# Gate and up weights of an expert block: one 2 MB request in place of two of 1 MB

## The reference, cut to what matters

```
def swiglu_2(t, w_gu, w_dn):
    g, u = jnp.split(t @ w_gu, 2, axis=-1)
    return (jax.nn.silu(g) * u) @ w_dn
...
    def one_block(args):
        rb, e = args
        return swiglu_2(t_pad[rb], w_gu[e], w_dn[e]).astype(jnp.float32)

    ys = lax.map(one_block, (rows.reshape(n_blk, EXPERT_BLOCK), blk_expert)).reshape(P, D)
```

## Time and profile before

| what | value |
|---|---|
| median of 3 runs | 3324.0 us (3318.94 to 3326.96) |
| profiled execution, its own time | 3329.74 us |
| span of the profiled execution | 3327.9 us |
| expert blocks | about 2560 to 3270 us of the span |
| requests of expert weights | 216 of 1 MB (72 for each of `big`, `h_buf`, `s_buf`) |
| DMA, whole span | 534.41 MB, mean 161 GB/s |
| TensorE clock granted | 0.994 of full speed |

### The profile page before, as it was taken

The page is one execution under the profiler, slowest core; times in us unless marked ns, Lnnn a source line. Parts: engine busy times, 40 slices in busy tenths (PEclk is TensorE's granted clock), DMA queues, the critical chain, the costliest instruction groups (busy, mean ns, idle before and its releaser), DMA issues.

```text
span 3327.9 us, 48518 instructions
## 1 busy us (share of the span) xinstructions
PE 3250.5 (98%) x16468; PEld 2622.7 (79%) x16468; DVE 1925.3 (58%) x2439; ACT 1720.2 (52%) x2077; POOL 1339.2 (40%) x675
## 2 busy tenths in 40 slices
PE   8999999999999999999999999999999999999997
PEld 7888887678888788888778888778766788887784
DVE  4335683663355433561473333456677899988897
ACT  5552334545533555321445542522453788888884
POOL 3444442044444344444234444434302444444441
PEclk9999999999999999999999999999999999999999
DMA  3224331022244222443422233223103999999997
GB/s 127 96 100 163 122 104 58 8 95 95 98 145 149 89 95 95 145 151 107 133 79 98 95 98 94 99 82 111 46 19 135 367 379 383 388 386 377 370 364 281
DMA packets 128451, 534.41 MB, mean 161 GB/s; under 512 B 24432, under 2 KB 24688, under 8 KB 100464
## 3 DMA queue, kind: packets, MB, share of 16 engines
q1 hardware_dynamic: 107488, 499.63, 42.5%
q0 software_dynamic: 20736, 33.60, 2.7%
q10 hardware_dynamic: 144, 0.08, 0.0%
HBM read 531.64 MB, written 41.94 MB: 172 GB/s over the span
## 4 chain that ended last, share of the span: by engine, by line
PE 50%; issue 33%; POOL 10%; DVE 3%; DMA 1%; ACT 1%; POOLq 0%; DVEq 0%; SPq 0%; ACTq 0%
PE ps L880 13%; PE ps L882 13%; PE ps L881 13%; POOL w_lo L2104 10%; PE ps L1451 2%; PE ps L1069 1%; PE ps L1094 1%; PE ps L1079 1%; PE ps L900 1%; PE ps L1543 1%; PE ps L1202 1%; PE ps L1240 1%; PE ps L1518 0%; DMA h_buf<-in_exp_gu 0%; PE ps L1470 0%
## 5 line engine op out<-in xcount | busy, mean ns | idle before, releaser
L2104 POOL TENSOR_TENSOR w_lo<-stage_buf,w_hi 128x1024 fp32r<-128x1024 f32 (+1 forms) x396 | 970.6, 2451 | 1478.0 <-ACT w_hi L1631 1477.9
L1631 ACT ACTIVATE w_hi<-stage_buf 128x1024 fp32r<-128x1024 f32 (+1 forms) x396 | 414.2, 1046 | 1178.8 <-PE ps L882 1125.6
L880 PE MATMUL ps<-x_hi,w_hi 128*128 128x512 f32 x1984 | 773.3, 390 | 4.5 <-POOL w_lo L2104 2.8
L882 PE MATMUL ps<-x_hi,w_lo 128*128 128x512 f32 x1984 | 772.0, 389 | 0.0
L881 PE MATMUL ps<-x_lo,w_hi 128*128 128x512 f32 x1984 | 771.9, 389 | 0.0
L880 PE MATMUL ps<-hid,w_hi 128*128 128x512 f32 x1312 | 518.5, 395 | 3.4 <-issue 1.7
L882 PE MATMUL ps<-hid,w_lo 128*128 128x512 f32 x1312 | 511.6, 390 | 0.0
L881 PE MATMUL ps<-hid,w_hi 128*128 128x512 f32 x1312 | 510.7, 389 | 0.0
L880 PEld LDWEIGHTS ps<-x_hi,w_hi 128*128 128x128 f32 x1984 | 372.4, 188 | 86.1 <-POOL w_lo L2104 4.9
L882 PEld LDWEIGHTS ps<-x_hi,w_lo 128*128 128x128 f32 x1984 | 372.4, 188 | 77.6
L881 PEld LDWEIGHTS ps<-x_lo,w_hi 128*128 128x128 f32 x1984 | 372.4, 188 | 76.9
(11 more groups left out here) (401 smaller groups left out, 4810.7 us busy)
## 6 DMA issues: line engine op xcount, KB each, us to landing
stage_buf<-in_gu SPq DMA_DIRECT2D x176, 512.0 KB, 3.2
big<-in_exp_gu SPq DMA_DIRECT2D x72, 1024.0 KB, 12.9
h_buf<-in_exp_gu SPq DMA_DIRECT2D x72, 1024.0 KB, 13.2
s_buf<-in_exp_dn SPq DMA_DIRECT2D x72, 1024.0 KB, 12.4
stage_buf<-in_down SPq DMA_DIRECT2D x64, 512.0 KB, 3.6
stage_buf<-in_down SPq DMA_DIRECT2D x32, 384.0 KB, 3.2
sil_buf<-in_ada SPq DMA_DIRECT2D x24, 512.0 KB, 4.1
tmp_buf<-in_ada SPq DMA_DIRECT2D x24, 512.0 KB, 4.2
```

The lines of the kernel that those rows point to most:

```text
L880: nc.tensor.matmul(o, a_hi, b_hi, start=start, stop=False)
L882: return nc.tensor.matmul(o, a_lo, b_hi, start=False, stop=stop)
L1631: nc.scalar.activation(w_hi[s][:, 0:n], stage[s][:, 0:n], ACT.Copy).then_inc(upper_done, 1)
L2104: nc.gpsimd.tensor_tensor(w_lo[s][:, 0:n], stage[s][:, 0:n], w_hi[s][:, 0:n].bitcast(F32), ALU.subtract).then_inc(parted, 1)
```

## The change

The two requests of a block's gate and up weights become one of 2 MB over the same bytes. It is issued after waiting for both halves to be split. ACT's waits for either half become a wait for the one semaphore. Buffers, order of the splits and everything on PE, DVE and POOL stay as they are.

```
-        raw_in = [[sem(f"raw_in{s}{j}") for j in range(3)] for s in range(2)]
+        raw_in = [[sem(f"raw_in{s}{n}") for n in ("gu", "dn")] for s in range(2)]
...
+        raw_gu = [big[:, 12288:16384], h_buf[:, :]]
...
-                    def load_raw(e, s, j):
-                        src = dr["exp_dn" if j == 2 else "exp_gu"][bass.ds(e, 1), :, :].rearrange("a p n -> p (a n)")
-                        sp.dma_start(raw[s][j], src if j == 2 else src[:, j * RAW:(j + 1) * RAW]).then_inc(raw_in[s][j], 16)
+                    def load_dn(e, s):
+                        sp.dma_start(raw[s][2], dr["exp_dn"][bass.ds(e, 1), :, :].rearrange("a p n -> p (a n)")).then_inc(raw_in[s][1], 16)
+
+                    def load_gu(e, s):
+                        sp.dma_start(raw_gu[s], dr["exp_gu"][bass.ds(e, 1), :, :].rearrange("a p n -> p (a n)")).then_inc(raw_in[s][0], 16)
...
-                    for j in range(2):
-                        load_raw(experts[0], 0, j)
-                    for j in range(2):
-                        load_raw(experts[1], 1, j)
+                    for s in range(2):
+                        load_gu(experts[s], s)
...
                         for j in range(2):
                             sp.wait_ge(raw_parted[j], s + 1)
-                            load_raw(e, s, j)
+                        load_gu(e, s)
...
                             e = expert_of(bass.ds(i * 2 + (s + 4), 1))
-                            sp.wait_ge(raw_parted[0], i * 2 + (s + 3))
-                            load_raw(e, s, 0)
-                            sp.wait_ge(raw_parted[1], i * 2 + (s + 3))
-                            load_raw(e, s, 1)
+                            for j in range(2):
+                                sp.wait_ge(raw_parted[j], i * 2 + (s + 3))
+                            load_gu(e, s)
...
-                        act.wait_ge(raw_in[s][j], landed)
+                        act.wait_ge(raw_in[s][j // 2], landed)
...
-                    act.wait_ge(raw_in[1][2], more_n * 16 + 32)
+                    act.wait_ge(raw_in[1][1], more_n * 16 + 32)
```

More of the change, by code:

```diff
@@ L721, in _ @@
                     experts = [expert_of(slice(b, b + 1)) for b in range(2)]
-                    for j in range(2):
-                        load_raw(experts[0], 0, j)
-                    for j in range(2):
-                        load_raw(experts[1], 1, j)
+                    for s in range(2):
+                        load_gu(experts[s], s)
                     sp.wait_ge(tab["in"], 2)
                     for s in range(2):
-                        load_raw(experts[s], s, 2)
+                        load_dn(experts[s], s)
                     for j in range(2):
@@ L739, in load_down @@
                         sp.wait_ge(raw_parted[2], i * 2 + (s + 1))
-                        load_raw(e, s, 2)
+                        load_dn(e, s)
                     with sp.Fori(0, more) as i:
```

## The result

| what | before | after |
|---|---|---|
| median of 7 executions (lowest to highest) | 3324.0 us (3318.94 to 3326.96) | 3333.93 us (3332.49 to 3341.14) |
| ratio, 95% interval | | 1.0036 (1.0026 to 1.0047) |
| profiled execution, its own time | 3329.74 us | 3340.68 us |
| its span | 3327.9 us | 3338.8 us |

The changed kernel is slower by 0.36%, some 12 us by the ratio; the two medians differ by 9.9 us. That is more than the 0.2% that a measurement can tell from no change. The time lies inside the range given, but outside the band that the prediction called "same" (up to 3330.6).

What follows compares the result with a forecast made beforehand. PE and the DMA engines were taken to run level in the expert loop, DMA setting its end. Terms +2.2 + 0 - 0.9 = +1.3 us on the median 3324.0 gave 3325.3 us, range 3315.6 to 3338.

Steps and rivals of the forecast that it cites:

- a serial cost per request: Weight requests: about 2 us fixed cost each, if serial, would bring some 144 us; the sum took nothing for it.
- Rival B: Saturated stretch: shorter queue lets uneven DMA engines run dry, PE idles more; +8.6 and +2.2, 3334.8 us; chance 0.19.
- Rival C: Expert blocks: gathers and scatters alternate with longer rows, so scatters miss their buffer's deadline; +14 us, 3338; chance 0.08.
- Fewer issues: SP's queue: one issue of 0.33 us less per block, nothing waiting behind it; 0.
- Later first half: Start of the expert stage: first half requested 2.2 us later, costing DMA only where its queue runs dry; +2.2 us.
- The lower limit: Expert loop: allowed landing time falls from 13.8 to 11.6 us, weight waits begin about 88 us earlier; 0, uncovered +2.2.
- cover: Loop's end: ACT's 4.9 us wait for the last down request, under which PE's 4.4 us delay fits.
- A queue before all 16 DMA engines: Expert stage: landing times growing from 6.7 to 13.8 us read as PE's demand outrunning DMA, 2.5 us per 100.
- Longer rows: Gate and up weights: 16 KB rows instead of 8 raise DMA throughput up to 0.5%; bounds 0 and -1.9, taken -0.9 us.
- Rival D: Expert loop: longer rows lift DMA over PE's demand, so the queue never fills; -8.4 us, 3315.6; chance 0.17.
- The signs: Profile after: 2 MB requests landing near 11.6 us, ACT's weight waits from near 2780, gathers 8.3, scatters 10.3 us.

Runs made afterwards that it cites:

- late_two_joint: late_two with ACT also waiting for both gate and up halves ahead of the first split; 3330.48 us, ratio 1.0021 to the kernel before.
- one_8k: The changed kernel with rows of 8 KB: one 2 MB request, weights laid out in DRAM as two halves; 3330.03 us, ratio 1.0020.
- late_two: The kernel before, with its two 1 MB requests of 8 KB rows both issued only once both halves are split; 3328.22 us, ratio 1.0014.
- before_halves: The kernel before with each gate and up half stored as a contiguous 1 MB in DRAM; 3325.18 us, ratio 1.0004.
- after_again: The changed kernel, unaltered, measured and profiled a second time beside later experiments; 3337.02 us, ratio 1.0038.
- one_4k: The changed kernel with 512 rows of 4 KB in its one 2 MB request; 3341.67 us, ratio 1.0060.
- scatter_late: one_8k with POOL holding each scatter until ACT's next split of a second half; 3371.74 us, ratio 1.0134.
- after_idx_ahead: The changed kernel with POOL copying the next block's table entry ahead of its waits, so gathers and scatters are requested earlier; 3336.9 us, ratio 1.0042.
- streams_busy: Separate kernel of transfers only, 8 KB rows: weights alone, with gathers and scatters, with 71 of 128 rows skipped; each with DVE and ACT idle, then busy; 1162.4 us.

## Why the prediction was right or wrong

**Where the loss would lie, and that it would be small: right.** The change costs 12 us; a serial cost per request would have made it a gain of 144, and the argument from several requests in flight held. (The 2 us that the prediction takes from the Trainium skill, DMA: Bandwidth & Descriptors, Anatomy of one DMA, are given there for requests that GpSimd (POOL) issues; these are SP's.) The loss is in the loop and at the stage's head. The range of 3315.6 to 3338 held the time, but the range owes its upper end to rivals B and C, with chances of 0.19 and 0.08. The sum itself moved by +1.3 us where the measured step is 10 to 12: that the time lies inside the range is luck as far as the sum goes.

**Fewer issues, 0: nothing against it.** No run isolates it, but late_two_joint (72 issues more) and one_8k agree in time, 1.0021 and 1.0020.

**Later first half, +2.2: not settled.** The part alone gave 1.0014, or +4.7 us, with an interval of +1.7 to +7.6. The upper bound of 2.2 lies inside that interval, so it is not refuted. The profile of late_two shows no loss at all in the stage, 765.0 us against 767.7. That a delay costs nothing more "once DMA is behind its former course" has one thing against it: DMA's share fell from 0.99 to 0.98 and 0.97. Whether that is a cost stays open, as its rate did not fall.

**The lower limit, 0 under a cover of 4.9 us: about +2 by the medians, 5.8 by the profiles.** The limit itself, 11.6, agrees with the landings: medians of 11.0 and 11.1, at most 12.5 and 12.4. The step to the joint wait raised the ratio from 1.0014 to 1.0020 and 1.0021, some 2 us, which is the price that the text gave "if the cover is gone" (+2.2). Adjacent intervals overlap, so this is an estimate from three medians. The profiles say 5.8 for the same step. In after the wait for the last down request is 2.8 us in place of 4.9, and the tail is shorter by the same 2.1: part of the cover was used. But the cover lies at the end, and it assumed that DMA, being always busy, would not notice what PE did. In one_8k DMA's share is down to 0.96 and 0.97, as if requests came late because splits come late. That is argued and not shown: the rate from 2870 us on did not fall (377 GB/s against 376), and PE's 5.5 us of idle time are no sign of loss, since before_halves, as fast as before, has 5.8.

**A queue before all 16 DMA engines: only in part what the landings meant.** The prediction read the landing times, 6.7 growing to 13.8 us, as a queue that PE's demand builds up before continuously busy DMA engines. The landings by parts say more. In before the first 15 of the 16 parts of a weight request stay within 2.1 to 3.5 us of each other all through the stage (medians). The last part lands 0.2 us behind them from 2600 to 2640 us, and 5.8 us behind them from 2870 on. So most of the growth is one part in sixteen that falls behind, and ACT has to wait for that one. In after_again it is 1.0 us behind.

**Longer rows, -0.9: wrong in sign, and this is the step that failed; it is about half of the loss.** Three kernels differ in the row length alone (and in the layout in DRAM, which made no difference in before_halves): one_8k (1.0020), after (1.0036 and 1.0038) and one_4k (1.0060). So 16 KB rows cost +5 to +6 us against 8 KB rows. The term was taken from throughput, and the throughput is as estimated or better: 426 against 422 GB/s. What the term left out is that gathers and scatters land later beside longer rows (scatters after 14.6 us, at 10.8 with rows of 8 KB). That was in the text as rival C, but as a case apart with a chance of 0.08, not as a term of the sum.

**Rival C, 0.08, 3338: the mechanism behind the rows' share of the loss.** Its landing times were good for the gather (11.1 against 11.6 measured) and short for the scatter (13.1 against 14.6, at the most 15.2 against 16.6). Its deadline of 14.4 us is below the measured median, so it is not a few of the slowest that are late. After waits 26 times and after_again 24 times among some 66 blocks, where a quarter was priced. The price was too high per hit: ACT waits 30.9 us for scatters, and PE is idle for 11.1 in all. That late scatters slow the kernel is shown by scatter_late; that they are the whole price of the rows is not, as after_idx_ahead says. "Whether a packet grows with the row no row here shows" was a fair statement of what was missing; but the argument for it, the narrow landings of the gathers beside growing ones of the weights, deserved more than 0.08.

**Rival B, 0.19, 3334.8: nearest in time, not the cause of the rows' share.** Its sign in the profile was given as PE idle over 8 us at a DMA share below 0.98, and after shows 11.7 us and 0.96 to 0.97. Yet pairs landing regularly over 11.6 us were to start it, and the median is 11.1. The same two numbers follow from late scatters. A sign that two mechanisms share decides nothing; the scatters' landing and the name of ACT's wait did. For the other half of the loss, that of late_two_joint and one_8k, B is not excluded: the share falls there too, ACT waits for weights, and the uneven landings that B asks for are there in before.

**Rival D, 0.17, 3315.6:** the landing did not stay below 10, and the rows brought 1% of rate, not 2.5.

**The signs.** Waits for weights begin at 2683 and not near 2780, and the waits for scatters at 2679, in the same stretch. The text expected 72 requests of 2 MB "each"; they are 36 and 36, 72 together.

What stays open: how the half of the loss that is not the rows' divides between the later first half and the joint wait, and by what way each costs time; and why after_idx_ahead, with most scatter waits gone, is no faster than after. No kernel tried was faster than the one before.

## What to carry to other kernels

A merged request is asked for as late as its last buffer and usable as late as its last byte; price both before counting the issue that is saved. When the rows of one queue get longer, look at the deadlines of the other queues: here 16 KB rows moved 1% more bytes per second by themselves, but the median scatter landed after 14.6 us in place of 10.3 to 10.8, past the 14.4 us that its buffer allowed. Before a landing time is read as a queue, ask whether all parts of the request are late or one. And a fall of two level resources at once points to a third thing that is late between them: name it by ACT's or DVE's waits, since PE's own may say only "issue".

## What was not expected of the hardware

- With the gate and up requests cut by partitions, 64 each (two_16k), the stage moves 198 GB/s at a DMA share of 1.00, against 377 in the kernel before.
- In before the last of a weight request's 16 parts falls behind the other 15, by 0.2 us at the start of the stage and by 5.8 us in its saturated stretch. Why one part lags, and whether it is always the same one, the trace does not tell.
- Skipping 71 of 128 rows as out of bounds did not shorten a block: 10.20 us against 9.97. Ten of the 16 parts of a weight request then land some 5 us ahead of the other six. The skipped rows do not vanish either. In the stretch from 760 to 900 us of streams_busy they show as small packets (2847 under 512 B, where the stretch from 360 to 500 has 896):

```profile
DMA packets 9833, 50.80 MB, mean 363 GB/s; under 512 B 2847, under 2 KB 2847, under 8 KB 4420
```

  By share they weigh more than their bytes: 363 GB/s at a share of 0.93 is 390 per full share, against 414 with all rows real and 383 in the kernel before (estimates from the rows of windows). The kernel gathers and scatters 72 blocks of 128 rows for 4096 real pairs, so skipped rows can explain part of why its share of 0.99 brings only 379 GB/s. That they do was not tried in the kernel.
- DVE and ACT at work in SBUF for 98% of the time take nothing from the DMA rate of the weights: 422 GB/s with and without.
